# First gate/up chunk in two 1 MB row groups, and two combinations moved one chunk later, in a streamed mixture-of-experts kernel

## The chip, the cores and the metric

The kernel runs on one core of a Trainium2 chip. The metric is the device time in microseconds (us), and lower is better. A run of it is the whole layer: one launch, all weights read from HBM.

## What is computed

The reference is one layer of a hybrid encoder over 256 prompt tokens and 64 sample tokens: a state-space mixer, a band attention, and then a mixture of experts in which each of the 320 tokens goes to 4 of 32 experts. All is fp32. The change lies in the mixture of experts:

```python
def expert_block(args):
    xb, e = args
    gu = xb @ w_gate_up[e] + b_gate_up[e]            # 1024 x 2048 weights, 8 MB an expert
    gate = jnp.minimum(gu[:, :D_FF], SWIGLU_LIMIT)
    up = jnp.clip(gu[:, D_FF:], -SWIGLU_LIMIT, SWIGLU_LIMIT)
    act = (up + 1) * gate * jax.nn.sigmoid(gate * SWIGLU_ALPHA)
    return act @ w_down[e] + b_down[e]               # 1024 x 1024 weights, 4 MB an expert
...
out = jnp.zeros_like(xt).at[sorted_tok].add(contrib)
```

## The kernel before

The first 300 us are the mixer, the attention and the router. Then `expert_pass` of the tensor engine runs 36 times. One pass takes one block of up to 64 tokens (CAP) through one expert. 32 experts have 36 blocks with these inputs: 28 experts have one pass, 4 have two passes in a row, and the order is made on the chip so that the doubled experts stand apart.

**The weights.** The ring has 6 slots of 2 MB, which is exactly one expert: gate/up chunks 0 to 3 (2 MB each, two row groups `kk` of 1 MB) and down chunks 4 and 5 (2 MB each). All are loaded by SyncE's queue (SP) in this order. In the loop over the experts `n`, SP waits before each chunk until TensorE has used the same chunk of the expert before in its last pass (`used[c]`: gs_used, gs_used1, gs_used2, gu_mm, ds_used, d_mm, each one higher per pass, against `first`, the number of passes before this expert). For a doubled expert this means that nothing is released in its first pass. Chunk 3 is already loaded by two transfers of 1 MB with two semaphores (w_full of its slot, and last_half_full), since the gate half of its products is made first, but both 1 MB transfers wait for the one gu_mm.

**One pass on TensorE**, in order: bias products (L1805); chunk 0 (16 matmuls, L1822); the combination of the block before for token tiles 0 and 1 (`combine(b - 1, 0)` and `(b - 1, 1)`, 8 matmuls, L1780), placed ahead of the chunk given by `outputs`; chunks 1 and 2; the gate half of chunk 3, the combination of token tile 2, the up half of chunk 3; the gather of the next block (L1748); transposes; chunks 4 and 5 (32 matmuls, L1862).

**VectorE in a pass:** `accumulate` of tiles 0 and 1 (4 scalar_tensor_tensor, L1145) after the combination; the one-hot matrices of the next block (L1118) and its selector (L1131, waits for gs_used); the gate clamp (L1230) after gate_mm, which begins the chain over ScalarE's sigmoid to the activation (L1237) for which the transposes of TensorE wait; `accumulate` of tile 2; and more.

The function `load` issues an unsplit chunk and has line 286 in the profile. L322 and L323 issue the two parts of chunk 3.

Of the kernel before, what the change touches and what calls it, by code (L numbers as in the profile page):

```python
# [18 lines left out]
NE, TOPK, F = 32, 4, 1024  # L19
# [25 lines left out]
GU_CHUNKS, DN_CHUNKS = 4, 2  # L45
EXPERT_SLOT = (1, 2, 3, 4, 0, 5)
# [12 lines left out]
def build(nc, x_prompt, x_sample, cache_k, cache_v, state_conv, state_ssm,  # L59
# [11 lines left out]
    with ctx:  # L71
# [3 lines left out]
        def sem(name):  # L75
            return ctx.enter_context(nc.semaphore(name))
# [111 lines left out]
        def low_part(t):  # L188
# [62 lines left out]
            gm_ready ed_ready m_ready xw_ready y_mm y_ev yb_free hst_mm hst_ev sout_out sqrt2 rec2 mixn turn_mm mixS_ready  # L251
            qk_mm mx_ready exp_ready pT_mm pT_ready pv_mm o_ready sqrt5 att_mm mixA_ready out_mm out_ev
            sqrt3 rstd_ready xn_ready hf_mm hf_dve hf_act lgp_mm pl_ready lgt_mm chosen_ready chosen01_ready rexp pv_ready pos_mm first_ready zeros_ready route_ready p_ready xe_mm ct_mm xe_ev
            xt_mm xt_ev gu_mm gate_mm gs_used gs_used1 gs_used2 ds_used g_ready sig_ready glu_ready up_ready act_ready
            comb_mm o_ev c_ready at_mm at_ev d_mm yy_ready turns_ready turns_mm order_ready bej_ready bej_mm b_hi brow_ready yyl_ready sel_ready rows_in up_in
            gates_ready gates_mm hi_ready mid_ready rest_ready xb_ready pcur_ready gates_held sqrt4 fin_ready y_out
            vchain achain pchain""".split()
        s = {n: sem(n) for n in names}
        last_half_full = sem("last_half_full")
        x_in = [sem(f"x_in{t}") for t in range(NT)]  # L260
        xres_in = [sem(f"xres_in{t}") for t in range(NT)]
        w_full = [sem(f"w_full{i}") for i in range(SLOTS)]
# [15 lines left out]
        def expert_arrival(c):  # L278

            return 16 * (len(range(EXPERT_SLOT[c], FRONT, FRONT_SLOTS)) if EXPERT_SLOT[c] < FRONT_SLOTS else 0) + 16  # L280
# [3 lines left out]
        def _(sp):  # L284
# [26 lines left out]
                wait_used(N_IN + j - FRONT_SLOTS)  # L311
                load(slot_of(N_IN + j), 4, wo[:, 4 * j:4 * j + 4, :])

            def load_expert(e, c):
                if c < GU_CHUNKS:
                    w, h, k0, k = w_gate_up[0], c // 2, 2 * (c % 2), 2
                else:
                    w, h, k0, k = w_down[0], c - GU_CHUNKS, 0, 4
                rows = w[bass.ds(e, 1)].rearrange("a (h p k) n -> p (a h) k n", h=2, p=128)
                if c == GU_CHUNKS - 1:  # L320
                    slot = ring[:, EXPERT_SLOT[c], :].rearrange("p (k n) -> p k n", k=k)
                    sp.dma_start(slot[:, 0:1, :], rows[:, h, k0:k0 + 1, :]).then_inc(w_full[EXPERT_SLOT[c]], 16)  # L322
                    sp.dma_start(slot[:, 1:2, :], rows[:, h, k0 + 1:k0 + 2, :]).then_inc(last_half_full, 16)  # L323
                else:
                    load(EXPERT_SLOT[c], k, rows[:, h, k0:k0 + k, :])
# [15 lines left out]
            with sp.Fori(1, NE) as n:  # L341
                e = sp.value_load(order[0:1, bass.ds(n, 1)], min_val=0, max_val=NE - 1)
                first = sp.value_load(before[0:1, bass.ds(n, 1)], min_val=1, max_val=MAX_BLOCKS)
                for c in range(GU_CHUNKS + DN_CHUNKS):

                    sp.wait_ge(s[used[c]], first)
                    load_expert(e, c)

            for t in range(2):
                sp.wait_ge(s["fin_ready"], t + 1)  # L350
# [919 lines left out]
        def _(pe):  # L1270
# [528 lines left out]
            def expert_pass(b, n, outputs, beside=None):  # L1799
# [7 lines left out]
                for c in range(GU_CHUNKS):  # L1807
                    if beside and c == 1:
                        tables_turned()
                    if beside and c == 2:  # L1810
                        gates_turned()
                        places(0)
                    if c == outputs:
                        combine(b - 1, 0)
                        combine(b - 1, 1)
                    pe.wait_ge(w_full[EXPERT_SLOT[c]], expert_arrival(c) + 16 * n)
                    w = ring[:, EXPERT_SLOT[c], :].rearrange("p (k n) -> p k n", k=2)

                    def gate_up(kk, m):
                        k = 2 * c + kk  # L1820
                        for h in range(2):
                            last = mm(PS[64 * h:64 * h + 64, m, :], xt[:, k % 4, k // 4, :],  # L1822
                                      w[:, kk, D * m + 512 * h:D * m + 512 * h + 512],
                                      start=False, stop=(k == KD - 1))
                        return last

                    if c < GU_CHUNKS - 1:
                        for kk in range(2):
                            for m in range(2):
                                last = gate_up(kk, m)  # L1830
                        last.then_inc(s[("gs_used", "gs_used1", "gs_used2")[c]], 1)
                    else:
                        for kk in range(2):
                            if kk == 1:
                                pe.wait_ge(last_half_full, 16 * n + 16)
                            last = gate_up(kk, 0)
                        last.then_inc(s["gate_mm"], 1)
                        combine(b - 1, 2)
                        for kk in range(2):
                            last = gate_up(kk, 1)  # L1840
                        last.then_inc(s["gu_mm"], 1)
# [36 lines left out]
            pe.wait_ge(s["zeros_ready"], 1)  # L1878
            total = pe.value_load(blocks[0:1, 0:1], min_val=NE, max_val=MAX_BLOCKS)
            with pe.Fori(1, total) as b:  # L1880
                expert_pass(b, pe.value_load(turn_of[0:1, bass.ds(b, 1)], min_val=0, max_val=NE - 1), outputs=1)
            for t in range(NT):
                combine(total - 1, t)

# [84 lines left out]
```

## Time and profile before

| | |
|---|---|
| median of 3 runs | 1292.07 us (1290.39 to 1294.35) |
| the profiled execution | 1290.63 us, its span 1288.7 us |
| TensorE busy | 1252.5 us, 97% of the span |
| mean granted TensorE clock | 0.996 |
| DMA | 436.33 MB, 339 GB/s over the span |
| expert passes | from 303 us to 1275 us of the span |

The busy share is that of the whole span. The windows, the waits and the chain tell more than it does, since a wait of a few tenths of a microsecond lies between busy stretches. A DMA row gives the time from the issue on SP to the landing of the last byte. In windows, DMA share is the mean of the 16 DMA engines, and GB/s what they moved.

### The profile page before, as it was taken

What the parts mean: (1) busy time and instruction counts of PE and PEld (TensorE: products, weight loads), DVE (VectorE), ACT (ScalarE), POOL (GpSimd) and SP (SyncE); (2) the same over time, 40 slices, a digit from 0 to 9 for tenths busy, and PEclk for the clock granted to TensorE, in tenths of its full rate; (3) what the DMA queues carried; (4) which work ended last, traced back from release to release, by engine and by line L of the source; (5) the groups of instructions that cost most, each with busy time, mean ns of one, the idle gap of its engine ahead of it and who ended that gap; (6) DMA issues with size and microseconds to landing.
All of it is one profiled execution on the core that took longest, in us unless ns stands there. A gap on an engine that the chain in (4) does not pass through costs nothing.

```text
span 1288.7 us, 17301 instructions
## 1 busy us (share of the span) xinstructions
PE 1252.5 (97%) x6444; PEld 549.3 (43%) x6445; DVE 490.8 (38%) x987; ACT 207.9 (16%) x407; POOL 36.9 (3%) x62
## 2 busy tenths in 40 slices
PE   7999999999999999999999999999999999999996
PEld 5755654664333343333333333333334333334332
DVE  2633444457533343333332333323334233233334
ACT  1131134452210010101101001110001010011102
POOL 2000003400000000000000000000000000000000
PEclk9999999999999999999999999999999999999998
DMA  9623126037999969999997999997999999699995
GB/s 321 219 77 121 66 82 214 25 132 292 421 426 427 428 276 426 427 430 426 429 419 290 427 428 427 427 427 307 398 427 428 427 428 426 284 428 428 426 426 201
DMA packets 48010, 436.33 MB, mean 339 GB/s; under 512 B 6229, under 2 KB 7373, under 8 KB 19318
## 3 DMA queue, kind: packets, MB, share of 16 engines
q1 hardware_dynamic: 43984, 429.41, 80.2%
q0 software_dynamic: 2080, 6.48, 1.5%
q10 hardware_dynamic: 1926, 0.18, 0.1%
q8 instruction: 13, 0.21, 0.1%
q14 instruction: 7, 0.06, 0.0%
HBM read 432.33 MB, written 3.72 MB: 338 GB/s over the span
## 4 chain that ended last, share of the span: by engine, by line
PE 85%; DMA 11%; DVE 2%; issue 1%; ACT 0%; POOL 0%; SPq 0%; DVEq 0%; POOLq 0%
PE PS L1822 34%; PE PS L1862 16%; DMA ring<-in_w_gate_up_dram 11%; PE PS L1320 7%; PE PS L1329 5%; PE PS L1275 5%; PE PS L1780 5%; PE PS L1748 4%; PE PS L1331 1%; PE PS L1617 1%; PE PS L1805 1%; PE PS L1591 1%; PE PS L1472 1%; PE PS L1458 1%; PE PS L1475 0%
## 5 line engine op out<-in xcount | busy, mean ns | idle before, releaser
L1822 PE MATMUL PS<-ring,r 128*64 128x512 f32 x2304 | 519.9, 596 | 11.5 <-DMA ring<-in_w_gate_up_dram 11.0
L1822 PEld LDWEIGHTS PS<-ring,r 128*64 128x64 f32 x2304 | 158.8, 137 | 314.1 <-issue 281.3
L1862 PE MATMUL PS<-ring,r 128*64 128x512 f32 x1152 | 255.1, 595 | 0.2
L1145 DVE SCALAR_TENSOR_TENSOR r<-PS,gprev,r 128x512 f32<-128x512 f32 (+1 forms) x222 | 152.5, 742 | 113.5 <-PE PS L1780 112.0
L1862 PEld LDWEIGHTS PS<-ring,r 128*64 128x64 f32 x1152 | 82.2, 137 | 148.2 <-issue 146.1
L1247 DVE TENSOR_TENSOR yy<-PS,yy 128x512 fp32r<-128x512 f32 x36 | 24.9, 692 | 249.6 <-ACT yy L736 249.6
L727 ACT ACTIVATE r<-r 128x512 f32<-128x512 f32 x36 | 22.7, 629 | 504.2 <-DVE r L1230 504.2
L1230 DVE TENSOR_SCALAR r<-PS 128x512 f32<-128x512 f32 x36 | 24.9, 692 | 202.3 <-PE PS L1822 202.3
L1275 PE MATMUL PS<-ident,r 128*128 128x128 f32 (+5 forms) x490 | 81.9, 298 | 10.1 <-DVE r L771 9.2
L1320 PE MATMUL PS<-r,ring 128*128 128x323 f32 x320 | 90.1, 438 | 0.0
L1275 PEld LDWEIGHTS PS<-ident,r 128*128 128x128 f32 (+5 forms) x490 | 62.7, 186 | 36.1 <-issue 18.2
L1780 PE MATMUL PS<-yy,place 64*128 64x512 f32 x444 | 71.8, 428 | 2.6 <-ACT yy L736 1.6
L1320 PEld LDWEIGHTS PS<-r,ring 128*128 128x128 f32 x320 | 60.5, 191 | 28.7 <-issue 3.7
L1780 PEld LDWEIGHTS PS<-yy,place 64*128 64x128 f32 x444 | 36.1, 186 | 65.6 <-issue 60.0
L736 ACT ACTIVATE yy<-PS 128x512 fp32r<-128x512 f32 x36 | 21.5, 597 | 261.2 <-PE PS L1862 261.2
L1748 PE MATMUL PS<-r,pm 128*64 128x512 bf16 x420 | 51.3, 379 | 0.0
L1329 PE MATMUL PS<-ring,r 128*128 128x512 f32 x96 | 42.1, 593 | 0.0
L1748 PEld LDWEIGHTS PS<-r,pm 128*64 128x64 bf16 x420 | 24.5, 110 | 34.8 <-issue 20.9
L732 ACT ACTIVATE r<-PS 128x512 f32<-128x512 f32 x36 | 21.5, 597 | 90.5 <-PE PS L1748 88.0
L1232 DVE TENSOR_TENSOR r<-r 128x512 f32<-128x512 f32 x36 | 24.9, 692 | 25.0 <-ACT r L727 25.0
L1234 DVE TENSOR_SCALAR r<-PS 128x512 f32<-128x512 f32 x36 | 24.9, 691 | 15.8 <-PE PS L1822 15.8
L1329 PE MATMUL PS<-ring 128*128 128x512 f32 x64 | 29.4, 603 | 1.1 <-DVE r L896 1.1
(317 smaller groups left out, 749.6 us busy)
## 6 DMA issues: line engine op xcount, KB each, us to landing
ring<-in_w_gate_up_dram SPq DMA_DIRECT2D x96, 2048.0 KB, 16.3
ring<-in_w_down_dram SPq DMA_DIRECT2D x64, 2048.0 KB, 16.6
ring<-in_w_gate_up_dram SPq DMA_DIRECT2D x64, 1024.0 KB, 16.3
ring<-in_w_in_dram SPq DMA_DIRECT2D x8, 2048.0 KB, 13.9
ring<-in_w_out_dram SPq DMA_DIRECT2D x3, 2048.0 KB, 7.6
r<-in_x_prompt_dram SPq DMA_DIRECT2D x2, 512.0 KB, 3.7
r<-in_x_prompt_dram POOLq DMA_DIRECT2D x2, 512.0 KB, 4.5
r<-bias_table_clipped SPq DMA_DIRECT2D x4, 256.0 KB, 7.0
```

The lines of the kernel that those rows point to most:

```text
L1145: v.scalar_tensor_tensor(xx, PS[0:rows, out_banks(t)[h], :], gprev[0:rows, t:t + 1], xx, ALU.mult, ALU.add)\
L1230: v.tensor_scalar(ug, bank(0), LIMIT, None, ALU.min).then_inc(s["g_ready"], 1)
L1232: v.tensor_tensor(sg, sg, ug, ALU.mult).then_inc(s["glu_ready"], 1)
L1234: v.tensor_scalar(uu, bank(1), LIMIT, -LIMIT, ALU.min, ALU.max).then_inc(s["up_ready"], 1)
L1247: v.tensor_tensor(yy2[:, 1, :], bank(2), yy2[:, 0, :].bitcast(f32), ALU.subtract)\
L1275: return nc.tensor.transpose(out, in_, ident[0:k, 0:k])
L1320: last = mm(PS[:, b, 0:HC], w[:, k, 128 * m:128 * m + 128], hT[:, k, :], start=(k == 0), stop=(k == KD - 1))
L1329: return mm(PS[:, b, :], lhs, rhs, start=first, stop=end)
L1748: last = mm(PS[64 * h:64 * h + 64, 3, :], pm[:, t, 64 * h:64 * h + 64], xb[t][:, part, 512 * h:512 * h + 512], start=(t == 0 and part == 0 ...
L1780: last = mm(PS[:, out_banks(t)[h], :], place[half, 128 * t:128 * t + 128], yy2[half, part, :], start=(part == 0), stop=(part == 1))
L1822: last = mm(PS[64 * h:64 * h + 64, m, :], xt[:, k % 4, k // 4, :], w[:, kk, D * m + 512 * h:D * m + 512 * h + 512], start=False, stop=(k = ...
L1862: last = mm(PS[64 * h:64 * h + 64, 2, :], at[:, kk, c, :], w[:, kk, 512 * h:512 * h + 512], start=(c == 0 and kk == 0), stop=(c == 1 and k ...
```

## The change

The load of chunk 0 is split in two transfers of 1 MB. The first goes out when TensorE has used row group 0 of the old chunk (new semaphore gs_half), the second when it has used all of it (gs_used). TensorE waits for the first on a new semaphore first_half_full before row group 0 and for the second on w_full before row group 1. In the loop over the passes 1 to 35, the combination of token tiles 0 and 1 stands ahead of chunk 2 (`outputs=2`) and no longer ahead of chunk 1. Pass 0 keeps it ahead of chunk 3.

```diff
+        first_half_full = sem("first_half_full")
...
-            def load_expert(e, c):
+            def load_expert(e, c, done=None):
...
-                if c == GU_CHUNKS - 1:
+                if done is not None and c > 0:
+                    sp.wait_ge(s[used[c]], done)
+                if c == 0:
+                    slot = ring[:, EXPERT_SLOT[c], :].rearrange("p (k n) -> p k n", k=k)
+                    if done is not None:
+                        sp.wait_ge(s["gs_half"], done)
+                    sp.dma_start(slot[:, 0:1, :], rows[:, h, k0:k0 + 1, :]).then_inc(first_half_full, 16)
+                    if done is not None:
+                        sp.wait_ge(s[used[c]], done)
+                    sp.dma_start(slot[:, 1:2, :], rows[:, h, k0 + 1:k0 + 2, :]).then_inc(w_full[EXPERT_SLOT[c]], 16)
+                elif c == GU_CHUNKS - 1:
...
                 for c in range(GU_CHUNKS + DN_CHUNKS):
-
-                    sp.wait_ge(s[used[c]], first)
-                    load_expert(e, c)
+                    load_expert(e, c, first)
...
-                    pe.wait_ge(w_full[EXPERT_SLOT[c]], expert_arrival(c) + 16 * n)
+                    if c == 0:
+                        pe.wait_ge(first_half_full, 16 * n + 16)
+                    else:
+                        pe.wait_ge(w_full[EXPERT_SLOT[c]], expert_arrival(c) + 16 * n)
...
                         for kk in range(2):
+                            if c == 0 and kk == 1:
+                                pe.wait_ge(w_full[EXPERT_SLOT[c]], expert_arrival(c) + 16 * n)
                             for m in range(2):
                                 last = gate_up(kk, m)
+                            if c == 0 and kk == 0:
+                                last.then_inc(s["gs_half"], 1)
...
-                expert_pass(b, pe.value_load(turn_of[0:1, bass.ds(b, 1)], min_val=0, max_val=NE - 1), outputs=1)
+                expert_pass(b, pe.value_load(turn_of[0:1, bass.ds(b, 1)], min_val=0, max_val=NE - 1), outputs=2)
```

## Rows read from the trace of the kernel before

**Rows 1.** The page: the span and TensorE's busy time.
```profile
span 1288.7 us, 17301 instructions
PE 1252.5 (97%) x6444; PEld 549.3 (43%) x6445; DVE 490.8 (38%) x987; ACT 207.9 (16%) x407; POOL 36.9 (3%) x62
```

**Rows 2.** Windows: stretch, us, busy by engine, PEclk, DMA share, GB/s.
```profile
468.29:685.29 217.00, 213.21 (x1114) 80.96 (x1114) 73.74 (x144) 22.39 (x40) 0.00 (x0) 1.00 0.96 406
685.29:902.69 217.40, 213.35 (x1114) 80.83 (x1114) 73.72 (x144) 22.39 (x40) 0.00 (x0) 1.00 0.96 405
1142.33:1248.00 105.67, 105.65 (x556) 40.50 (x554) 36.86 (x72) 11.06 (x20) 0.00 (x0) 1.00 1.01 427
677.00:686.00 9.00, 9.00 (x48) 3.30 (x44) 0.89 (x2) 0.60 (x1) 0.00 (x0) 1.00 0.00 0
686.00:688.00 2.00, 2.00 (x12) 0.70 (x12) 2.00 (x4) 0.00 (x0) 0.00 (x0) 1.00 0.95 262
```

**Rows 3.** Waits: PE and PEld from 464 to 1119 us, SP 685 to 712.
```profile
PE PS L1822 <- DMA ring<-in_w_gate_up_dram: 11.0, 15, 1.2
...
PEld PS L1822 <- DMA ring<-in_w_gate_up_dram: 26.6, 23, 2.1
...
PEld PS L1275 <- DVE r L1237: 9.9, 24, 0.4
...
SPq L286 <- PE PS L1822: 40.2, 4, 31.2
```

**Rows 4.** The chain from 610 to 682 us: start, us, what.
```profile
613.74 24.17 DMA ring<-in_w_gate_up_dram
...
642.26 25.08 DMA ring<-in_w_gate_up_dram
```

**Rows 5.** Timeline of SP's queue, second pass of the expert doubled at 652 us.
```profile
685.29 8.47 SPq L286 DMA_DIRECT2D ring<-in_w_gate_up_dram  x3
...
690.00 0.33 SPq L286 DMA_DIRECT2D ring<-in_w_gate_up_dram  x1
...
697.68 0.33 SPq L322 DMA_DIRECT2D ring<-in_w_gate_up_dram  x1
...
704.50 3.77 SPq L286 DMA_DIRECT2D ring<-in_w_down_dram  x2
...
711.80 8.47 SPq L286 DMA_DIRECT2D ring<-in_w_gate_up_dram  x3
```

**Rows 6.** Landings of issues at 685.29, 690.00, 704.50, 473.00, 487.49, 921.89; us last.
```profile
ring<-in_w_gate_up_dram SPq DMA_DIRECT2D x1, 2048.0 KB, 7.3
...
ring<-in_w_gate_up_dram SPq DMA_DIRECT2D x1, 2048.0 KB, 8.1
...
ring<-in_w_down_dram SPq DMA_DIRECT2D x1, 2048.0 KB, 8.4
...
ring<-in_w_gate_up_dram SPq DMA_DIRECT2D x1, 2048.0 KB, 7.6
...
ring<-in_w_down_dram SPq DMA_DIRECT2D x1, 2048.0 KB, 8.0
...
ring<-in_w_down_dram SPq DMA_DIRECT2D x1, 2048.0 KB, 8.1
```

**Rows 7.** Timeline of TensorE in the same pass.
```profile
681.50 3.61 PE L1822 MATMUL PS<-ring,r 128*64 128x512 f32 x16
685.04 1.19 PE L1780 MATMUL PS<-yy,place 64*128 64x512 f32 x8
686.16 8.80 PE L1822 MATMUL PS<-ring,r 128*64 128x512 f32 x40
```

**Rows 8.** Timeline of VectorE in the same pass, idle time before in brackets.
```profile
685.80 2.73 DVE L1145 SCALAR_TENSOR_TENSOR r<-PS,gprev,r 128x512 f32<-128x512 f32 x4 [3.19 <-PE PS L1780]
...
689.36 0.19 DVE L1131 CAST sel<-row_of 128x64 bf16 x1
695.02 0.69 DVE L1230 TENSOR_SCALAR r<-PS 128x512 f32<-128x512 f32 x1 [5.47 <-PE PS L1822]
```

More of the change, by code:

```diff
@@ L253, in build @@
             sqrt3 rstd_ready xn_ready hf_mm hf_dve hf_act lgp_mm pl_ready lgt_mm chosen_ready chosen01_ready rexp pv_ready pos_mm first_ready zeros_ready route_ready p_ready xe_mm ct_mm xe_ev
-            xt_mm xt_ev gu_mm gate_mm gs_used gs_used1 gs_used2 ds_used g_ready sig_ready glu_ready up_ready act_ready
+            xt_mm xt_ev gu_mm gate_mm gs_half gs_used gs_used1 gs_used2 ds_used g_ready sig_ready glu_ready up_ready act_ready
             comb_mm o_ev c_ready at_mm at_ev d_mm yy_ready turns_ready turns_mm order_ready bej_ready bej_mm b_hi brow_ready yyl_ready sel_ready rows_in up_in
```

## The prediction

> **What bounds the kernel now.** I read the page first: TensorE is busy for 1252.5 of 1288.7 us [rows 1], so what is left to gain by better timing of loads is small and must be found in stretches. The queue of SP gives the stretches. In an expert with two passes nothing is released in the first, so SP pauses there. The issues of chunk 0 in the second passes of the doubled experts stand at 468.29, 685.29, 902.69 and 1119.69 us, and I cut the expert stage there. The windows of two of these three cycles are 217.00 and 217.40 us, and the third is again 217.00 [rows 2]. Each has 8 passes and loads 7 experts.
>
> A pass that waits for nothing takes 711.80 - 685.29 = 26.51 us, from chunk 0 issue to chunk 0 issue [rows 5]. The stretch of four passes after the last cycle has TensorE busy for 105.65 of 105.67 us [rows 2]. Eight such passes are 212.1 us, so a cycle loses 4.9, 5.3 and 4.9 us, 15.1 us in all. The waits say what the loss is: from 464 to 1119 us TensorE's matmuls and weight loads wait for gate/up chunks, 11.0 and 26.6 us in total, which overlap each other [rows 3]. The chain says where: in the last two experts of the cycle it leaves TensorE and runs for 24.17 and 25.08 us along the transfer of the last 1 MB of chunk 3, until 667.34 us [rows 4]. The reader is to see that this is a long queue, not a slow transfer: 2 MB pass in 2.097 MB / 428 GB/s = 4.9 us, an expert in 29.4 us, against 26.51 us of TensorE. DMA falls back by 2.9 us a pass, and eats up over five passes the lead that it got in the doubled pass.
>
> So the time at which a cycle ends is the time at which its DMA work begins, plus seven experts of transfer less the last two down chunks. The lead is not fully used: from 677 to 686 us DMA moves nothing [rows 2], because all six slots are full until the second pass of the doubled expert gives up chunk 0. **What the kernel can gain is an earlier start of DMA after that pause, three times, as long as nothing behind it in the queue runs dry.** The fourth pause, at 1119 us, is followed by five passes that never wait for DMA, and gains nothing.
>
> **Part 1, chunk 0 released by row groups.** In a long group 40 matmuls of this form take 8.80 us [rows 7], 0.22 us each, so the second 8 matmuls of chunk 0 take 1.7 us (1.76 with the tail of the group in it). The first 1 MB can be issued at 685.29 - 1.7 = 683.6 us [rows 5]. SP is waiting there already: its wait for chunk 0 in this pass is 31.2 us long [rows 3], so no instruction ahead of it on its queue delays it. A transfer into the idle queue lands 7.3 us after its issue [rows 6]: 4.9 us of transfer and 2.4 us that do not scale with it, by subtraction. I use landing = later of (landing before, own issue + 2.4 us) + transfer, with 2.45 us for 1 MB. The first half lands at 688.4, the second, issued at 685.29, lands at 690.9: 1.7 us ahead of the 692.6 of before (685.29 + 7.3). One more issue on SP is 0.33 us of a queue that waits anyway.
>
> **Part 2, the combination one chunk later.** Chunk 1 was issued at 690.00 [rows 5]. Its 2.4 us make 692.4, just before chunk 0's landing at 692.6, so with part 1 alone the queue would run dry for 1.5 us. The 8 combination matmuls take 686.16 - 685.04 = 1.12 us [rows 7]; behind chunk 1 they release it at 688.9, which with 2.4 us is 691.3. So it lands at 696.2, 1.9 us earlier than the 698.1 of before [rows 6]. The matmuls are the same, with one change to the combination's form and one back either way, so TensorE pays nothing. Chunk 2 is issued as before, at 685.29 + 8.47 - 0.33 = 693.43 (the third of the merged issues, [rows 5]), and is no limit: it could start at 695.8, before 696.2.
>
> **What the moved work delays.** VectorE's accumulation starts 3.4 to 3.5 us later, the time of chunk 1's 16 matmuls: its work from 685.80 to 689.55 becomes 689.2 to 693.0. The next that TensorE needs of it is the gate clamp at 695.02, before which it idles for 5.47 us [rows 8]. That leaves 2.0 us. This cover is worth guarding: the transposes of TensorE wait already for the activation at the end of that chain, 0.4 us of weight load in each pass [rows 3], so any lateness beyond 2.0 us would be paid once a pass. One-hot matrices and selector are used only after chunk 3 and in the next pass. ScalarE waits for the combination of tile 2, which stays. Both new waits of TensorE are met long before in a pass without DMA delay. The wait in the middle of chunk 3 shows their price: 40 matmuls over three chunks and this wait stand in one row of 8.80 us without idle time, 0.22 us each, as against 3.61 / 16 = 0.23 in chunk 0's group alone [rows 7]. I take zero.
>
> **Does the 1.7 us last?** Follow the queue. Chunk 3 was issued at 697.68, and could start at 700.1, while its predecessor landed at 698.1 + 4.9 = 703.0: 2.9 us to spare, enough. Chunk 4 is issued at 704.50, when half of the down products are made; nothing in the change moves that [rows 5]. It landed after 8.4 us [rows 6]. An issue into an empty queue takes 7.3 us. So it can gain 8.4 - 7.3 = 1.1 us and no more: with a head start of 1.7 us DMA runs dry there for about 0.6 us. In the cycles from 468 and 902 us chunk 4 landed after 8.0 and 8.1 us [rows 6], so 0.7 and 0.8 us are left. After chunk 4 the backlog grows and no limit comes again: the next chunk 0 is issued at 711.80 and lands over 10 us later.
>
> What does a chunk need whose queue is nearly, but not quite, empty? The trace does not have the case itself. From above, chunk 1 is the nearest: issued 2.5 us before its predecessor landed, it took 7.6 and 8.1 us [rows 6], where the rule gives 7.4. With their mean, 7.85, the gains would be 0.15, 0.55 and 0.25, 0.95 us in all. From below, 7.3 gives 0.7 + 1.1 + 0.8 = 2.6 us. I take 7.4, near the lower end, because chunk 1 follows directly on the slow first two microseconds (262 GB/s, [rows 2]) and chunk 4 does not: 0.6 + 1.0 + 0.7 = **2.3 us**. The lost 4.9 us a cycle is more than this, so all of it counts.
>
> The Trainium skill, DMA: Bandwidth & Descriptors, section "Anatomy of one DMA", has a fit for another issue path: 2.0 us fixed plus bytes / 436 GB/s, an estimate of 6.8 us for 2 MB. This trace's shortest are 7.2 and 7.3 us. By the page's figure chunk 4 would gain 1.2, 1.6 and 1.3 us, 4.1 us in all, instead of 2.3.
>
> **Sum.** Profiled execution: 1290.63 - 2.3 = 1288.3 us. Its own time is 1.4 us under the median of the runs, so against the median: 1292.07 - 2.3 = **1289.8 us**, 0.18% less. The measurement can tell about 0.3% (3.9 us) from no change.
>
> **Rivals.**
> (A) The forecast, chance 0.55: 1289.8, own range 1288.0 to 1291.3.
> (B) The queue that is not quite empty has no such floor, 0.20. In the first two microseconds after the pause DMA moves 0.52 MB where 428 GB/s would be 0.86 MB; that is 0.8 us. If this belongs to the restart alone, chunk 4's floor is 6.5 us, its margins are 1.5, 1.9 and 1.6, capped at 1.7 by the head start: 4.8 us, 1287.3. Against it: chunk 1's 7.6 to 8.1 us behind a queue that was not empty. The page's figure above ends in this case too.
> (C) The gain is lost nearly wholly, 0.15: each near-empty handover costs 0.4 us or more, as chunk 1's did, and two more small transfers only shift bubbles. 0 to 0.95 us, 1291.6.
> (D) Slower, 0.10: VectorE's accumulation comes late for the gate clamp. It decides from 2.0 us of extra lateness on, for instance if its four reads of PSUM slow down beside the products of chunk 2. There are 29 passes bound by TensorE with the moved combination; 0.3 us beyond the slack costs 8.7 us, less 2.3: 1298.5. To be slower by over 0.3% it needs 6.2 / 29 = 0.21 us a pass. Against it: the same four instructions run beside chunk 1's products today at 2.73 us.
>
> The range reaches from (B), with 1.5 us for the scatter of medians, to (C) with the same: 1285.8 to 1293.0. Faster: (B) and about an eighth of (A), 0.27. Slower: (D), 0.10. Within 0.3%: the rest, 0.63.
>
> **What the profile after would show.** The first 1 MB issue about 1.7 us before the second, and chunk 1 issued 3.5 us after that. Chunk 4 landing 7.3 to 7.5 us after an issue that keeps its place in the pass. A dip of DMA for half a microsecond just before it. Cycles of 216.4, 216.4 and 216.3 us in place of 217.0, 217.4 and 217.0. VectorE idle 2.0 us before the gate clamp, and passes without waits still 26.51 us. The prediction is wrong if chunk 4 lands in under 7 us, if the cycles shrink by over 1.3 us each, or if 26.51 grows.

## The result, and the profile after

The change made the kernel slower: 1299.89 us, median of 6 runs (1297.32 to 1302.75), against 1291.50 us, median of 6 runs of the kernel before (1290.39 to 1294.35). The ratio is 1.0058, 95% interval 1.0045 to 1.0071. The forecast was 1289.8 us. The profiled execution of after took 1302.75 us, with a span 12.0 us longer than before. It was the slowest of the six, so the accounts below explain 12.0 us, where the medians are 8.4 us apart.

The page after [rows 1 before]:
```profile
span 1300.7 us, 17395 instructions
PE 1258.1 (97%) x6444; PEld 549.8 (42%) x6445; DVE 490.5 (38%) x987; ACT 207.9 (16%) x407; POOL 37.0 (3%) x62
```
TensorE has the same 6444 matmuls and is busy 5.6 us longer. Nearly all of this is a lower clock, three times 1.7 us in the three cycles, as shown below; but most of it falls into stretches in which TensorE would have waited for DMA anyway.

Windows of after, cut at the issue of the second half of chunk 0, which has the place of the chunk 0 issue of before [rows 2]; then four short stretches:
```profile
470.27:690.80 220.53, 214.99 (x1114) 81.56 (x1112) 73.70 (x144) 22.40 (x40) 0.00 (x0) 0.99 0.96 399
690.80:910.13 219.33, 214.98 (x1114) 81.55 (x1112) 73.69 (x144) 22.40 (x40) 0.00 (x0) 0.99 0.96 402
910.13:1129.97 219.84, 214.82 (x1114) 81.57 (x1112) 73.69 (x144) 22.40 (x40) 0.00 (x0) 0.99 0.96 401
662.36:665.77 3.41, 3.41 (x10) 0.97 (x10) 0.00 (x0) 0.00 (x0) 0.00 (x0) 0.50 0.98 413
680.00:689.00 9.00, 9.00 (x46) 3.22 (x44) 1.08 (x2) 0.60 (x1) 0.00 (x0) 1.00 0.01 5
492.00:495.00 3.00, 3.00 (x18) 1.13 (x16) 0.69 (x1) 0.60 (x1) 0.00 (x0) 1.00 0.94 319
```
The three cycles grew from 217.0, 217.4 and 217.0 us to 220.5, 219.3 and 219.8: 8.3 us of the 12.0. Each now loses 7.2 to 8.4 us against eight passes of 26.51 us, where it lost 4.9 to 5.3. DMA rests from 680 to 689 us as before. Some 24 us after the end of the first such pause (492 to 495 us) it moves only 319 GB/s for three microseconds, before it has got back into its stride of 427 GB/s. And there is something that before did not have: 3.41 us in which TensorE's granted clock is 0.50, its level of 1.2 GHz.

SP's queue in the second pass of the expert doubled at 657 us [rows 5 before]:
```profile
689.08 0.34 SPq L327 DMA_DIRECT2D ring<-in_w_gate_up_dram  x1
690.80 0.33 SPq L330 DMA_DIRECT2D ring<-in_w_gate_up_dram  x1
694.22 5.05 SPq L287 DMA_DIRECT2D ring<-in_w_gate_up_dram  x2
...
703.19 0.33 SPq L333 DMA_DIRECT2D ring<-in_w_gate_up_dram  x1
703.70 0.33 SPq L334 DMA_DIRECT2D ring<-in_w_gate_up_dram  x1
710.01 3.77 SPq L287 DMA_DIRECT2D ring<-in_w_down_dram  x2
...
715.60 0.34 SPq L327 DMA_DIRECT2D ring<-in_w_gate_up_dram  x1
```
All issues stand where the prediction put them: the first 1 MB 1.72 us ahead of the second, chunk 1 3.42 us behind that, and the next pass 715.60 - 689.08 = 26.52 us later, so a pass that waits for nothing costs what it did. The landings of these issues [rows 6 before], in order of 689.08, 690.80, 694.22, 698.94, 703.19, 703.70, 710.01 and 713.44 us:
```profile
ring<-in_w_gate_up_dram SPq DMA_DIRECT2D x1, 1024.0 KB, 5.2
...
ring<-in_w_gate_up_dram SPq DMA_DIRECT2D x1, 1024.0 KB, 7.1
...
ring<-in_w_gate_up_dram SPq DMA_DIRECT2D x1, 2048.0 KB, 9.0
...
ring<-in_w_gate_up_dram SPq DMA_DIRECT2D x1, 2048.0 KB, 9.5
...
ring<-in_w_gate_up_dram SPq DMA_DIRECT2D x1, 1024.0 KB, 7.7
...
ring<-in_w_gate_up_dram SPq DMA_DIRECT2D x1, 1024.0 KB, 9.7
...
ring<-in_w_down_dram SPq DMA_DIRECT2D x1, 2048.0 KB, 9.9
...
ring<-in_w_down_dram SPq DMA_DIRECT2D x1, 2048.0 KB, 11.3
```
This is where the gain is lost. Put the landings in order and subtract what a transfer takes in a steady stream (4.9 us for 2 MB, 2.45 for 1 MB). "Lead" is how long a transfer had been issued when the one before it landed. The change from one transfer to the next is a handover below, and a queue with a lead of only a few microseconds is called thin:

| transfer | issue | landing | since the landing before | lead | lost |
|---|---|---|---|---|---|
| chunk 0, first 1 MB | 689.08 | 694.28 | | | 0.4 (5.2, against 4.8) |
| chunk 0, second 1 MB | 690.80 | 697.90 | 3.6 | 3.5 | 1.2 |
| chunk 1 | 694.22 | 703.22 | 5.3 | 3.7 | 0.4 |
| chunk 2 | 698.94 | 708.44 | 5.2 | 4.3 | 0.3 |
| chunk 3, both | 703.70 | 713.40 | 5.0 | 4.7 | 0.1 |
| chunk 4 | 710.01 | 719.91 | 6.5 | 3.4 | 1.6 |
| chunk 5 | 713.44 | 724.74 | 4.8 | 6.5 | 0 |

4 us are lost between the first issue and the landing of chunk 5. The queue never ran empty here: by the rule of the prediction, 2.4 us of lead are enough. In the kernel before, the same stretch is 685.29 to 707.93 + 9.9 = 717.8, 32.5 us; here it is 35.7. The head start of 1.7 us is gone, and 1.4 us more.

Two views for the other engines. Waits of after, from 300 to 1290 us:
```profile
PEld PS L1834 <- DMA ring<-in_w_gate_up_dram: 36.8, 27, 2.8
...
DVE r L1239 <- PE PS L1834: 78.0, 35, 2.9
...
PE PS L1834 <- DMA ring<-in_w_gate_up_dram: 15.8, 17, 1.9
```
VectorE in the pass of 689 us [rows 8 before]:
```profile
694.75 2.73 DVE L1154 SCALAR_TENSOR_TENSOR r<-PS,gprev,r 128x512 f32<-128x512 f32 x4 [6.63 <-PE PS L1789]
...
698.31 0.19 DVE L1140 CAST sel<-row_of 128x64 bf16 x1
700.53 0.69 DVE L1239 TENSOR_SCALAR r<-PS 128x512 f32<-128x512 f32 x1 [2.03 <-PE PS L1834]
```
VectorE idles 2.03 us before the gate clamp, as forecast (2.0), and its four reads take the same 2.73 us. What grew is TensorE's wait for gate/up chunks.

### Where each cycle went

I cut a cycle in three: **A**, from the first issue after the pause to the landing of chunk 5 of that pass; **B**, from there to the landing of the last 1 MB of chunk 3 of the seventh expert; **C**, from there to the first issue after the next pause. For the cycle from 689.08 us of after, B ends at 867.76 + 24.4 = 892.16 us (the landing below) and C at the issue at 908.41.
```profile
ring<-in_w_gate_up_dram SPq DMA_DIRECT2D x1, 1024.0 KB, 24.4
```
Means over the three cycles, in us, of the kernels that are explained below. "A less head start" sets the first early issue aside: it tells when chunk 5 landed, counted from the moment at which TensorE gave up all of chunk 0. The tail is the time from the fourth pause's first issue to the end of the span. A, B and C rest on landings that the profile prints to 0.1 us, and are good to that.

| kernel | A | A less head start | B | C | cycle | tail | median us |
|---|---|---|---|---|---|---|---|
| before | 32.27 | 32.27 | 166.92 | 17.94 | 217.13 | 169.0 | 1291.50 |
| after | 35.79 | 34.07 | 167.33 | 16.79 | 219.90 | 172.4 | 1299.89 |
| comb_only | 32.00 | 32.00 | 166.94 | 17.95 | 216.89 | 169.0 | 1291.78 |
| split_only | 35.00 | 33.28 | 167.38 | 16.23 | 218.60 | 171.4 | 1294.61 |
| split_late | 32.01 | 32.01 | 167.41 | 17.93 | 217.35 | 168.9 | 1293.72 |
| start_late | 31.78 | 35.2 | 167.41 | 21.65 | 220.84 | 167.9 | 1306.77 |
| half_12 | 34.00 | 33.14 | 167.42 | 17.07 | 218.49 | 169.8 | 1296.45 |
| comb_parts | 35.64 | 33.92 | 167.33 | 16.21 | 219.18 | 172.7 | 1300.13 |
| c4_half | 34.29 | 32.57 | 167.71 | 16.74 | 218.73 | 170.2 | 1294.13 |
| halves_014 | 34.65 | 32.93 | 168.12 | 16.55 | 219.32 | 171.3 | 1297.47 |
| gap_full | 34.45 | 32.73 | 167.46 | 16.22 | 218.13 | 170.7 | 1295.22 |
| halves_014_12 | 32.26 | 31.40 | 168.17 | 17.05 | 217.49 | 169.6 | 1292.72 |
| gap_mid_c4 | 34.38 | 32.66 | 167.75 | 16.17 | 218.30 | 170.2 | 1294.14 |

From before to after, A grew by 3.52 us, B by 0.41 and C shrank by 1.15: 2.77 us a cycle, 8.3 in three. The tail grew by 3.4, of which 1.7 are the head start itself, so by 1.7 net; the remaining 2.0 us of the 12.0 lie ahead of the first pause. That front part differs from execution to execution (the first issue after the first pause stands between 465.6 and 471.7 us in kernels whose front is the same), and I put nothing of it down to the change. One part of it is visible: in after the clock stands at the lower level for 3.4 us from 269.8 us on, ahead of the expert passes, and 8 matmuls take 5.20 us there in place of 3.63. half_12, gap_full and gap_mid_c4 show the same near 270 us; before, comb_only and split_only don't.

### The profile page after: what moved, and what is told of

It reads as the page before. It is cut to its first block, busy times and chain, and to the rows that moved or that the text cites. A ratio compares the mean times of both kernels' runs of the same rounds, so it can differ in the third digit from the quotient of the medians.

```text
span 1300.7 us, 17395 instructions
## 1 busy us (share of the span) xinstructions
PE 1258.1 (97%) x6444; PEld 549.8 (42%) x6445; DVE 490.5 (38%) x987; ACT 207.9 (16%) x407; POOL 37.0 (3%) x62
## 4 chain that ended last, share of the span: by engine, by line
PE 76%; DMA 20%; DVE 2%; ACT 1%; issue 1%; POOL 0%; ACTq 0%; SPq 0%; DVEq 0%; POOLq 0%
PE PS L1834 31%; DMA ring<-in_w_gate_up_dram 19%; PE PS L1878 14%; PE PS L1329 5%; PE PS L1338 5%; PE PS L1284 4%; PE PS L1789 4%; PE PS L1757 3%; PE PS L1340 1%; PE PS L1626 1%; DMA dsk<-in_d_skip_dram 1%; PE PS L1814 1%; PE PS L1600 1%; PE PS L1481 1%; PE PS L1467 1%
```

## The experiments

All kernels compute the whole layer; none leaves work out. A ratio is to the kernel before, with its 95% interval.

### First: which of the two parts, and is it the early start?

**comb_only** is the kernel before with the combination moved, and nothing else:
```diff
-                expert_pass(..., outputs=1)
+                expert_pass(..., outputs=2)
```


> Only the combination of tiles 0 and 1 is moved behind chunk 1; chunk 0 is loaded whole, as before. Theory 1 (two separate costs: restarts of single DMA engines after the pause, made by the early first 1 MB; and TensorE clock drops, made by the moved combination, because the wait for chunk 1 becomes one uninterrupted idle of 1.9 us): chunk 1 is issued 1.1 us earlier, DMA side unchanged or up to 0.5 us a cycle better (217.0 to 216.5 us), but up to three stretches of half clock of 3.4 us, each worth up to 1.7 us: 1288 to 1296 us. Theory 2 (the 1 MB transfers with their 8 KB runs slow DMA): as the kernel before, 1290 to 1292, no clock drops. If chunk 4 lands later than 8.5 us after its issue here, the move alone upsets DMA and theory 1 is wrong in that part.

Measured: 1291.78 us, 0.9997 (0.9983 to 1.0010); cycles of 216.9 us, no stretch at half clock. The combination alone is free, and its stretches at half clock, which I had expected, did not come.

**split_only** is after with the combination left in its place:
```diff
-                expert_pass(..., outputs=2)
+                expert_pass(..., outputs=1)
```


> Only the load and the release of chunk 0 by 1 MB halves; the combination stays ahead of chunk 1. Theory 1: no clock drop (the combination parts the waits), but the DMA engines fall out of step after each pause as in the changed kernel: chunk 4 lands about 10 us after its issue, cycles of 218.5 to 220 us, in all 1295 to 1299 us. Theory 2 (transfer size): the same time, so this run does not part the two. Rival 3 (the moved combination is the whole cause): 1288 to 1291 us.

Measured: 1294.61 us, 1.0018 (1.0005 to 1.0030). This is just under the 1295 to 1299 expected. A is 35.00 us, 1.0 us worse than before once the head start is set aside. Chunk 4, issued at 706.91 us, took 9.2 us with nothing moved around it, against 8.0 in comb_only:
```profile
ring<-in_w_down_dram SPq DMA_DIRECT2D x1, 2048.0 KB, 9.2
```

**split_late** keeps the two transfers and takes the early issue away. Both wait for all of chunk 0:
```diff
-                        sp.wait_ge(s["gs_half"], done)
+                        sp.wait_ge(s[used[c]], done)
                     sp.dma_start(slot[:, 0:1, :], ...)
```


> As the changed kernel, but both 1 MB halves of chunk 0 are issued behind gs_used, so the first no longer goes out early. Theory 1: the 16 DMA engines restart once, stay in step, chunk 4 lands 8.0 to 8.5 us after its issue, cycles near 217, perhaps with clock drops: as comb_only, 1288 to 1296 us. Theory 2: the small transfers are still there, so chunk 4 lands after about 10 us and the time stays at 1297 to 1303 us.

Measured: 1293.72 us, 1.0016 (1.0002 to 1.0030). Its landings for the issues at 685.76, 686.28, 689.18 and 704.96 us:
```profile
ring<-in_w_gate_up_dram SPq DMA_DIRECT2D x1, 1024.0 KB, 4.8
...
ring<-in_w_gate_up_dram SPq DMA_DIRECT2D x1, 1024.0 KB, 6.7
...
ring<-in_w_gate_up_dram SPq DMA_DIRECT2D x1, 2048.0 KB, 8.7
...
ring<-in_w_down_dram SPq DMA_DIRECT2D x1, 2048.0 KB, 7.9
```
The second half lands at 692.98, 7.2 us after the first issue, as one 2 MB transfer does. Chunk 4 is back at 7.9 us and A at 32.01. So neither the split nor the moved combination makes the loss in A: it needs the early issue. What the split costs by itself is in B, 0.4 to 0.5 us a cycle.

**start_late** turns the question round. Both halves wait until chunk 1 has been used, 3.4 us later than in split_late:
```diff
-                        sp.wait_ge(s["gs_half"], done)
+                        sp.wait_ge(s[used[1]], done)
```


> As the changed kernel, but both halves of chunk 0 wait until chunk 1 too is used, so 4 MB are issued at once 5.3 us later than the first 1 MB of the changed kernel. If only the time at which DMA starts counted, each of three cycles would grow by 5.3 us: about 1315 us. Theory 1: with 4 MB behind the restart no engine runs dry, chunk 4 lands about 1.4 us later than in the changed kernel: at most 4 us over it, 1300 to 1304 us, with the spread of the 16 completion writes of a transfer back at 0.5 us.

Measured: 1306.77 us, 1.0121 (1.0092 to 1.0149), above the expected 1300 to 1304. A is the cleanest of all, 31.78 us. C grows by 3.4 us over before in the first two cycles (21.4 against 18.0), and by 4.3 in the third, in which TensorE's clock fell (1104.9 us): the time at which DMA begins does set the cycle's end, one for one. That part of the prediction's model holds. The 16 DMA engines finish chunk 5 within 0.4 to 0.5 us of each other, as expected. A cycle is 220.84 us, only 0.9 longer than in after.

**half_12** gives half the head start, 0.86 us: the old row group is used up by the first 8 matmuls, but the release comes after 12.
```diff
-                            if c == 0 and kk == 0:
-                                last.then_inc(s["gs_half"], 1)
+                                if c == 0 and kk == 1 and m == 0:
+                                    last.then_inc(s["gs_half"], 1)
```


> As the changed kernel, but the first 1 MB goes out after 12 of the 16 matmuls of chunk 0, so the two halves are issued 0.86 us apart and no longer 1.72. Theory 1 (each of the 16 DMA engines that reaches the end of its queue, even for a moment, restarts with a loss of 1 to 1.6 us, and every later landing waits for the slowest engine): the second half comes in time, so nothing is lost at chunk 0 or 1, but chunk 4, whose lead is at most 0.3 us beyond its need, still loses 1.5 us in some engines: cycles of 217.3 to 218.3 us, 1292 to 1296 us. If instead the loss grows with the head start alone, half of it goes: cycles of 218.3 us at chunk 0 and 1 too, 1295 to 1297 us.

Measured: 1296.45 us, 1.0038 (1.0025 to 1.0052). The expectation was that chunks 0 and 1 would lose nothing; chunk 1 lost 0.9 us (8.7 us from its issue at 690.00 us). With half the head start A is still 0.9 us worse than before, head start aside. So a smaller head start alone does not avoid the loss.

### Second: the clock

TensorE in after, at 656 to 669 us, the first pass of the doubled expert:
```profile
656.64 3.61 PE L1834 MATMUL PS<-ring,r 128*64 128x512 f32 x16
...
662.18 5.35 PE L1834 MATMUL PS<-ring,r 128*64 128x512 f32 x16 [1.93 <-DMA ring<-in_w_gate_up_dram]
667.46 1.20 PE L1789 MATMUL PS<-yy,place 64*128 64x512 f32 x8
```
The same work in comb_only:
```profile
655.96 3.65 PE L1822 MATMUL PS<-ring,r 128*64 128x512 f32 x16 [0.39 <-DMA ring<-in_w_gate_up_dram]
...
660.85 3.65 PE L1822 MATMUL PS<-ring,r 128*64 128x512 f32 x16 [1.24 <-DMA ring<-in_w_gate_up_dram]
```
When DMA sets the pace, TensorE has to wait somewhere. In comb_only it waits 0.39 us before chunk 0 and 1.24 before chunk 1. With the halves it can start chunk 0 at once, and with the combination gone from between the chunks nothing fills the gap, so it stands for 1.93 us in one piece. Right behind it 16 matmuls take 5.35 us in place of 3.65, at a granted clock of 0.50. This came at 662.4, 853.5 and 1102.7 us of after.

**comb_parts** is after with the combination of tile 0 put back ahead of chunk 1, and that of tile 1 left ahead of chunk 2, so that each gap has half of the filler:
```diff
+                    if c == (3 if beside else 1):
+                        combine(b - 1, 0)
                     if c == outputs:
-                        combine(b - 1, 0)
                         combine(b - 1, 1)
```


> As the changed kernel, but the combination of tile 0 stays ahead of chunk 1 and that of tile 1 goes ahead of chunk 2, so that the 1.9 us for which TensorE waits for chunk 1 in the passes bound by DMA is cut in two by 4 matmuls. Theory on the clock: no stretch of half clock in the expert stage; the DMA losses stay, cycles near 219 us, 1295 to 1299 us. If the clock falls all the same, the uninterrupted wait is not what it follows.

Measured: 1300.13 us, 1.0057 (1.0035 to 1.0079), just above its range. The filler works: the wait shrinks to 1.26 us and no stretch at half clock comes in any cycle.
```profile
660.30 0.73 PE L1789 MATMUL PS<-yy,place 64*128 64x512 f32 x4
...
662.29 3.65 PE L1835 MATMUL PS<-ring,r 128*64 128x512 f32 x16 [1.26 <-DMA ring<-in_w_gate_up_dram]
```
C falls from 16.79 to 16.21 us, and the median doesn't improve. In after the drops cost 0.8 us in each of the two cycles where they hit the last pass (C of 17.06 and 17.05 against 16.25 in the third); in the third it was absorbed. The clock is real, shown, and too small for 8 us. A stays 35.64: the losses of DMA are still there (chunk 4 issued at 709.62 us took 10.2).

### Third: where in the queue

**c4_half** is after with chunk 4 also released and loaded by halves, so that the queue gets work 1.7 us sooner where it was thinnest:
```diff
+                elif c == GU_CHUNKS:
+                    sp.wait_ge(s["ds_half"], done)
+                    sp.dma_start(slot[:, 0:2, :], rows[:, h, 0:2, :]).then_inc(down_half_full, 16)
+                    sp.wait_ge(s[used[c]], done)
+                    sp.dma_start(slot[:, 2:4, :], rows[:, h, 2:4, :]).then_inc(w_full[EXPERT_SLOT[c]], 16)
```


> As the changed kernel, and chunk 4 too is released and loaded by 1 MB halves, the first 1.72 us earlier. Theory 1: chunk 4's first half arrives while all engines still have work, so the 1.5 to 2.0 us lost there go: cycles of 217.6 to 218.8 us, 1293 to 1297 us. If small transfers as such disturb DMA, one more split makes it slower: over 1300 us.

Measured: 1294.13 us, 1.0022 (1.0011 to 1.0033). The cycles were 218.4 to 219.3 us, where 217.6 to 218.8 was expected. A falls from 35.79 to 34.29 us: chunk 4's halves lose nothing, where chunk 4 of after lost 1.5 to 2.0 us. It is not all gained, since in two of three cycles chunk 2 or 3 now loses 1.8 to 2.1. B pays 0.4 for one more transfer.

**halves_014** is c4_half with chunk 1 halved in the same form. With every handover up to chunk 2 better fed, a loss by a thin queue should have gone:
```diff
+                if c in half_full:                          # chunk 1
+                    sp.wait_ge(half_used[c], done)
+                    sp.dma_start(slot[:, 0:m, :], ...).then_inc(half_full[c], 16)
+                    sp.wait_ge(s[used[c]], done)
+                    sp.dma_start(slot[:, m:2 * m, :], ...).then_inc(w_full[EXPERT_SLOT[c]], 16)
```

> As c4_half, and chunk 1 by 1 MB halves as well, so every handover near which an engine can run dry, except that inside chunk 0, has 1.7 us more. Theory 1: what is left is the loss of 0.7 to 1.0 us at the second half of chunk 0, against a start 1.72 us earlier than in the kernel before: cycles of 216.2 to 217.2 us, shorter waits that do not let the clock fall, 1289 to 1292 us, level with the kernel before or a little faster. If transfer count were the cause: the slowest of all.

Measured: 1297.47 us, 1.0040 (1.0027 to 1.0054), and the cycles were 218.2, 219.6 and 220.1 us where 216.2 to 217.2 was expected. A is no better than in c4_half. The loss had moved to chunk 2, issued at 693.62 us with a lead of 3.4 us; it lost 10.6 - 3.4 - 4.9 = 2.3 us:
```profile
ring<-in_w_gate_up_dram SPq DMA_DIRECT2D x1, 2048.0 KB, 10.6
```

**gap_full** is the sharpest run. It is after with the second half of chunk 0 held back until chunk 1 has been used, 3.4 us later. The early 1 MB then goes through alone, DMA stops, and starts again with a full second half and chunk 1 right behind it. By any account in which DMA only needs work sooner, this is slower than after.
```diff
                     if done is not None:
-                        sp.wait_ge(s[used[c]], done)
+                        sp.wait_ge(s[used[1]], done)
                     sp.dma_start(slot[:, 1:2, :], ...)
```


> As the changed kernel, but the second 1 MB of chunk 0 waits until chunk 1 is used too, 3.4 us later than in the changed kernel. The queue then runs wholly empty between the two halves. If lateness as such costs, this is the slower: the landing of chunk 5 after the pause comes up to 3.4 us later than in the changed kernel (35.6 to 36.2 us after the first issue), 39 us. Theory 1 in its sharper form (an empty queue costs only its gap; the loss comes from handovers in which some of the 16 engines are just running out): chunk 5 lands by the times of start_late less 1 MB, 35.2 + 1.7 - 2.45 = 34.5 us after the first issue, 1.1 to 1.7 us sooner than in the changed kernel though issued later; cycles of 218.1 to 219.0 us, 1293 to 1298 us.

SP's queue and the landings of the issues at 686.40, 691.55, 692.07, 707.32 and 710.75 us:
```profile
686.40 0.34 SPq L327 DMA_DIRECT2D ring<-in_w_gate_up_dram  x1
691.55 0.33 SPq L330 DMA_DIRECT2D ring<-in_w_gate_up_dram  x1
692.07 4.52 SPq L287 DMA_DIRECT2D ring<-in_w_gate_up_dram  x2
707.32 3.77 SPq L287 DMA_DIRECT2D ring<-in_w_down_dram  x2
```
```profile
ring<-in_w_gate_up_dram SPq DMA_DIRECT2D x1, 1024.0 KB, 4.7
...
ring<-in_w_gate_up_dram SPq DMA_DIRECT2D x1, 1024.0 KB, 4.8
...
ring<-in_w_gate_up_dram SPq DMA_DIRECT2D x1, 2048.0 KB, 9.1
...
ring<-in_w_down_dram SPq DMA_DIRECT2D x1, 2048.0 KB, 8.7
...
ring<-in_w_down_dram SPq DMA_DIRECT2D x1, 2048.0 KB, 10.1
```
Measured: 1295.22 us, 1.0025 (1.0015 to 1.0035), faster than after. The second half goes out 3.4 us later, and chunk 5 lands sooner: 34.45 us after the first issue in place of 35.79, with 34.5 expected. The stop costs 691.55 - 691.10 = 0.45 us and the 2.4 of a restart, 2.85 us; 12 MB without any loss are 2.4 + 6 x 4.9 = 31.8, and 31.8 + 2.85 = 34.65 already covers the 34.45 measured. Nothing else was lost. In after there is no stop, and 4.0 us are.

**halves_014_12** is halves_014 with the release of half_12: a smaller head start, and small transfers behind it.
```diff
-                            if c < 2 and kk == 0:
-                                last.then_inc(s["gs_half"] if c == 0 else half_used[c], 1)
+                                if c == 0 and kk == 1 and m == 0:
+                                    last.then_inc(s["gs_half"], 1)
+                            if c == 1 and kk == 0:
+                                last.then_inc(half_used[c], 1)
```

> As halves_014, but the first 1 MB goes out after 12 of the 16 matmuls. The candidate with the most lead at every handover and still a head start of 0.86 us. Theory 1: no handover near the edge before chunk 2, chunk 5 lands 32.1 to 33.5 us after the first issue; with three more transfers an expert the middle of a cycle takes 168.1 us; cycles of 217.3 to 218.5 us, 1290 to 1295 us: no gain over the kernel before. A cycle under 216.5 us would say that the split can be made to pay.

Measured: 1292.72 us, 1.0007 (0.9993 to 1.0020), within its range. A less head start is 31.40, the only kernel clearly under before (32.27). Here the early start paid 0.9 us a cycle in A, and B took 1.25 back. That is the best of the versions with early halves, and no faster than before.

**gap_mid_c4** is c4_half with the second half of chunk 0 released in the middle of chunk 1, where DMA has just finished the first: a clean restart with a shorter gap.
```diff
                     if done is not None:
-                        sp.wait_ge(s[used[c]], done)
+                        sp.wait_ge(s["gs_half1"], done)     # after the first 8 matmuls of chunk 1
```


> As c4_half, but the second 1 MB of chunk 0 is issued after the first 8 matmuls of chunk 1: 3.4 us after the first 1 MB and 1.7 us later than in the changed kernel. By then the first has wholly left the queue, so all 16 engines restart together; chunk 1 follows with a lead of 3 us, chunk 4 with 3.7 us. Theory 1: no loss but the gap; chunk 5 lands 32.6 us after the first issue (33.8 to 34.6 in c4_half, though issued sooner there), the middle of a cycle takes 167.7 us, and cycles are 216.5 to 217.3 us, 1289 to 1293 us. If lateness as such costs, cycles are over 218.5 us, as c4_half or longer.

Measured: 1294.14 us, 1.0011 (1.0000 to 1.0022); cycles of 218.2 to 218.4 us where 216.5 to 217.3 was expected, and the time above its 1289 to 1293. The second half restarts cleanly (4.8 us), but chunk 1, issued 1.7 us behind it with a lead of 3.1, lost 0.6 to 1.1 us, and chunk 2 up to 1.0. My idea that engines which have started together stay together is not the whole rule.

### Fourth: is it the count of transfers or the size of their runs?

**part_split** is split_late with chunk 0 divided by partitions, 64 and 64, so that each partition's run is 16 KB again and not 8:
```diff
-                    sp.dma_start(slot[:, 0:1, :], rows[:, h, k0:k0 + 1, :])
+                    sp.dma_start(slot[0:64, :, :], rows[0:64, h, k0:k0 + 2, :])
...
-                    sp.dma_start(slot[:, 1:2, :], rows[:, h, k0 + 1:k0 + 2, :])
+                    sp.dma_start(slot[64:128, :, :], rows[64:128, h, k0:k0 + 2, :])
```


> As split_late (both transfers of chunk 0 behind gs_used), but each carries 64 partitions with both row groups, in runs of 16 KB, and TensorE waits for both before chunk 0. Measures the 0.4 to 0.5 us by which the six experts in the middle of a cycle became slower to stream with one more transfer each (166.9 to 167.4 us from chunk 5 of the first to the last half of chunk 3 of the seventh). If it is the number of transfers: 167.4 again. If it is the 8 KB runs: 166.9. In all 1290 to 1294 us.

Measured: 1463.71 us, 1.1327 (1.1284 to 1.1371). It answers another question. Windows, the first with these transfers in flight and the second with ordinary ones:
```profile
546.00:552.00 6.00, 6.00 (x31) 2.40 (x32) 1.16 (x3) 0.48 (x1) 0.00 (x0) 1.00 0.94 221
526.00:530.00 4.00, 4.00 (x22) 1.43 (x20) 0.69 (x1) 0.60 (x1) 0.00 (x0) 1.00 0.99 414
```
A transfer to 64 partitions moves at 221 GB/s, half of 414, with all DMA engines shown busy; 1 MB takes 4.7 to 5.0 us in the stream, and each of 32 experts pays some 5 us. The Trainium skill, SBUF — State Buffer, section "Door 1: The DMA port swizzle", says that 64 partitions reach only 8 of the 16 ports, about 218 GB/s; the trace agrees with 221. Whether B grows by the count of transfers or by their 8 KB runs stays open.

## Why the prediction was wrong

**Right.** The first 1 MB went out 1.72 us sooner (1.7 forecast), chunk 1 3.42 us after the release of chunk 0 (3.5), VectorE was left 2.03 us (2.0), and the undisturbed pass kept its 26.52 us. So rival (D) fails in its mechanism: VectorE's accumulation was never late, though the sign and nearly the size (1298.5) were those of (D). The model that a cycle ends when its DMA work began plus its transfers also held where nothing else changed: start_late moved the start by 3.4 us, and C by 3.4 in the two cycles without a fall of the clock. Rival (B) fails too: chunk 4 came later than 7.3 us, and not sooner. Rival (C) had the kind of loss right, but let it take the gain and no more.

**The step that failed: "Does the 1.7 us last?"** It took 7.4 us for chunk 4 behind a nearly empty queue, and let every other transfer start whenever it had been issued 2.4 us before its turn. Chunk 4 landed 10.3, 9.9 and 9.7 us after its issue, in the three cycles. The prediction's rule gives a loss only for a lead under 2.4 us. Over all handovers in the passes after a pause, of all kernels but part_split, what was lost beyond that rule is:

| kernels | lead | handovers | lost over 0.35 us |
|---|---|---|---|
| chunk 0 at once (before, comb_only, split_late, start_late) | 2 to 3 us | 9 | 3, by 0.4 to 0.6 |
| | 3 us and more | 95 | none |
| early first 1 MB (the nine others) | 2 to 3 us | 38 | 32, mean of all 0.9, longest 2.9 |
| | 3 to 4 us | 62 | 29, mean of all 0.6 |
| | 4 to 5 us | 50 | 7, mean of all 0.1 |
| | 5 us and more | 114 | none |
| | under 2 us (queue runs out, by the rule) | 12 | none |

The counts use landings to 0.1 us. With the unrounded times of the traces the third, fourth, fifth and sixth rows are 29 of 36, 30 of 63, 7 of 52 and none of 113.

The same lead of 3 to 4 us is free where the queue began with 2 MB at once and costs 0.6 us on average where it began with an early 1 MB. It is not the lead alone, though: gap_full, in which DMA stops behind the early 1 MB, lost nothing in any handover, and halves_014_12 only in one of its 16 with that lead.

The single packets of split_only show what differs. For chunk 4, issued at 488.41 us, 14 of the 16 DMA engines wrote their completion from 495.1 to 495.9 us and the last two at 497.0 and 497.2. In comb_only all 16 wrote within 0.4 us. The lateness is made at the handover: from 490.5 to 491.5 us only 13 or 14 packets are in flight, though chunk 4 was issued over 2 us before, and then two packets that begin at 491.54 and 491.61 us take 1.16 and 1.37 us, where 0.61 is usual. By their times they are the late engines' first packets of chunk 4; the trace does not number the engines. In comb_only there are never fewer than 15 in flight from 474.5 to 679 us.

A landing is that of the slowest engine, and the late engines do not catch up behind a full queue. In split_only the 16 completions of a transfer lie 2.0 us apart from chunk 4 on and still 1.9 us at 679.5 us, the last landing of the cycle; the next pause brings them together again (0.35 us). In after they lie 2.3 to 2.4 us apart from 720 to 902 us, in comb_only 0.6 us. So the whole cycle runs on the times of the late engines. At the landing of chunk 5 the spread is 0.4 to 1.1 us in the six kernels whose A shows little loss beyond their later start or their stop (before, comb_only, split_late, start_late, gap_full, halves_014_12), and 1.2 to 3.2 us in the other seven.

Most of the lateness comes from slow packets and less from engines without one. From 2.8 to 33 us after each first issue, as a mean over the 16 engines, packets took 1.8 to 2.4 us more than usual in after and engines stood without a packet for 0.4 to 0.7 us; in comb_only it is at most 0.13 and 0.03 us. That is as far as the records go. Why such slow packets come in passes with an early first 1 MB, and why half_12, halves_014 and gap_mid_c4 lost at other places than expected, was not settled. The Trainium skill, DMA: Bandwidth & Descriptors, section "Why a DMA increments its semaphore by 16 and not by 1", says that the up to 16 engines of a DMA finish independently and only the full count means that all has landed; this trace agrees, with completions of one transfer from 495.1 to 497.2 us.

Where I erred in reading: I took one landing time (7.4 us) as a property of an empty queue, from rows in which the queue had just been filled with 2 MB. Chunk 1's 8.1 us [rows 6] was the warning, and rival (C) named it, but priced it at "0.4 us or more" and capped the loss at the head start. Measured are 4.0 us of losses in A (35.8 less the 31.8 that 12 MB take without any), where the forecast comes to 1.4 (0.5 that before has already, and 0.95), in a stretch where I had allowed for none but chunk 4's.

**Sizes, per cycle.** The forecast was -0.77 us, the result +2.77; the difference of 3.5 us is:
- 2.6 us in A, which the prediction let grow by 0.95 (1.72 less 0.77) and which grew by 3.52. This is the main term. comb_parts has the same A and the same median without any stretch at half clock; split_late, with the same transfers and no early issue, has none of it.
- 0.4 us in B. "One more issue on SP is 0.33 us of a queue that waits anyway" was right for SP and wrong for DMA. With one more transfer an expert B is 167.3 to 167.5, with two 167.7, with three 168.1 to 168.2, from 166.9: some 0.4 us a cycle each, 0.07 us an expert. comb_only, without the split, stays at 166.94.
- 0.6 us in C, from the clock, in two of three cycles. In these runs it came only with both parts of the change together: neither comb_only nor split_only has a wait over 1.3 us before those matmuls, nor a drop. It does not come each time: half_12 has six waits of 1.92 to 1.94 us and no drop in its expert passes. The prediction had no step for the clock.

**The tail.** "The fourth pause ... gains nothing" should have said: and loses as well. The tail grew by 1.7 us net of the head start, and two waits for chunks stand in it that before had not, 0.65 us at 1262.99 and 0.46 at 1272.86. They account for 1.1 of the 1.7.

**What undoing the parts gives.** Without the moved combination 1.0018, without the early issue 1.0016, with chunk 4 halved 1.0022, with chunks 1 and 4 halved and a later release 1.0007, and with the combination alone 0.9997. None beats before. The parts of the change are not additive: comb_only and split_only sum to +0.15%, together they are +0.58%. In terms of the table, A less head start is 32.0 and 33.3 us apart and 34.1 together. The moved combination brings chunk 1 forward, and spaces the issues of chunks 0 and 1 by 3.4 us, so more handovers fall into the band of 3 to 4 us. That is an argument from the table, not a run of its own.

## What to carry to other kernels

Before bringing a transfer forward into an idle queue, follow the lead of every transfer behind it (landing of the one before, less its issue). If the head start makes several leads of 2 to 4 us, the early start can cost more than it brings; letting DMA stop and restart with a full queue was better here, even 3.4 us later (gap_full against after). A loss made at one handover stayed until the next pause here, because the late engines did not catch up. Price a split on DMA's side, not only on the issuing queue's, by comparing a long streaming stretch with and without it. And look at what a moved piece of TensorE work had been filling: two waits of 0.4 and 1.2 us that merge into one of 1.9 can bring the clock down.

## What the runs showed of the hardware

- **A queue that is never empty can lose 1 to 3 us in one handover.** With an early 1 MB, 32 of 38 handovers with a lead of 2 to 3 us lost over 0.35 us, and chunk 4 took 9.2 to 10.5 us in split_only and after, where 2 MB take 7.1 to 7.3 from a full stop.
- **DMA engines that fall out of step stay out of step while the queue is full:** in split_only the 16 completions of a transfer lay 2.0 us apart at 498 us and 1.9 us at 680 us, and 0.35 us after the next stop.
- **A restart from a full stop is clean.** 1 MB landed in 4.6 to 4.9 us after 45 of 48 stops (all kernels but part_split; 5.0 to 5.3 us after the other three, in after and split_only) and 2 MB in 7.1 to 7.3, also 0.5 us after the queue has run out (gap_full, 691.55 us: 4.8).
- **More transfers cost streaming time even in a deep queue:** 0.07 us each, read from B over six experts.
- **TensorE's clock fell behind waits of 1.83 to 2.08 us.** Of 44 waits of 1.8 to 2.1 us in the expert stage (part_split aside), 12 were followed by about 3.4 us at the lower level (1.2 GHz); behind shorter waits, of up to 1.6 us, none was.
- **Half the partitions, half the rate:** 221 GB/s for transfers to 64 partitions against 414.
